# One-hots for the gate matrices, made token by token instead of eight tokens at a time

## What is computed

```
s = einsum('nhpc,hpkc->nhpk', q, sub_keys)            # two sides of 128 scores
ts, ti = top_k(s, 16)
cand_s = ts[:, :, 0, :, None] + ts[:, :, 1, None, :]
cand_i = ti[:, :, 0, :, None] * 128 + ti[:, :, 1, None, :]
best_s, best_p = top_k(cand_s, 16)
idx = take_along_axis(cand_i, best_p)
gate = softmax(best_s)
act = gelu(einsum('nd,nhkd->nhk', x, u[idx]))
out = einsum('nhk,nhkd->nd', gate * act, v[idx])
```

## Time and profile before

| | |
|---|---|
| median of 3 runs | 2251.53 us |
| the profiled execution | 2253.01 us, span 2251.7 us |
| PE busy | 2114.5 us (94%) |
| DVE busy | 1506.8 us (67%) |
| ACT busy | 879.1 us (39%) |
| POOL busy | 714.2 us (32%) |
| DVE instructions | 2554 |
| mean granted clock of PE | 0.971 of 2.4 GHz |

### The profile page before, as it was taken

One profiled execution on the slowest core, in us unless ns is written; L12 is line 12 of the kernel. 1 busy time (PEld: TensorE's weight loads), 2 busy tenths in 40 slices (PEclk: granted clock), 3 DMA queues, 4 the chain that ended last, 5 costly groups with the idle time before them and its releaser, 6 DMA issues.

```text
span 2251.7 us, 31360 instructions
## 1 busy us (share of the span) xinstructions
PE 2114.5 (94%) x12750; PEld 1228.8 (55%) x12827; DVE 1506.8 (67%) x2554; ACT 879.1 (39%) x1057; POOL 714.2 (32%) x540
## 2 busy tenths in 40 slices
PE   6999999999999979999999999999789898999998
PEld 5464664555566646666655555555445464444444
DVE  4557644798989899996788888888674374332002
ACT  5333542333243337675333333333232464434110
POOL 2311001311334342223233333343336302555440
PEclk9999899999999989999999999999799998999999
DMA  6223571226898888889999999999422201322310
GB/s 208 75 75 114 183 266 38 95 75 220 301 340 303 311 301 291 333 326 349 376 373 378 384 372 383 381 381 371 155 75 99 75 20 38 112 92 95 150 38 38
DMA packets 194479, 483.39 MB, mean 215 GB/s; under 512 B 10672, under 2 KB 93648, under 8 KB 188320
## 3 DMA queue, kind: packets, MB, share of 16 engines
q1 hardware_dynamic: 154624, 334.65, 41.5%
q0 software_dynamic: 39712, 146.74, 17.3%
HBM read 428.92 MB, written 52.43 MB: 214 GB/s over the span
## 4 chain that ended last, share of the span: by engine, by line
PE 50%; DVE 28%; DMA 15%; issue 3%; ACT 2%; POOL 1%; SPq 1%; DVEq 0%; ACTq 0%; POOLq 0%
PE psum L568 13%; PE psum L569 13%; PE psum L567 13%; DMA expert_act<-act_dram 12%; DVE weight_low L2060 6%; DVE row_sum L2301 2%; POOL weight_low L2634 1%; DVE hidden_low L2480 1%; DVE expert_act L2475 1%; DVE gated_one_hot_b L2460 1%; DVE one_hot_b L2457 1%; PE psum L788 1%; DVE one_hot_a L2454 1%; DVE rows_a L2288 1%; PE psum L882 1%
## 5 line engine op out<-in xcount | busy, mean ns | idle before, releaser
L567 PE MATMUL psum<-x_high,weight_high 128*128 128x384 bf16 (+3 forms) x1825 | 632.0, 346 | 22.5 <-DVE weight_low L2060 17.2
L568 PE MATMUL psum<-x_low,weight_high 128*128 128x384 bf16 (+3 forms) x1845 | 639.7, 347 | 11.1 <-DVE x_low L1938 5.9
L569 PE MATMUL psum<-x_high,weight_low 128*128 128x384 bf16 (+3 forms) x1844 | 638.7, 346 | 0.6
L1330 ACT ACTIVATE weight_high<-weight_stage 128x4096 bf16<-128x4096 f32 (+2 forms) x100 | 356.3, 3564 | 243.3 <-DMA weight_stage<-peer_v_dram 120.7
L2634 POOL TENSOR_TENSOR weight_low<-weight_stage,weight_high 128x512 bf16<-128x512 f32 (+1 forms) x229 | 300.8, 1348 | 426.2 <-ACT weight_high L1330 426.2
L567 PE MATMUL psum<-hidden_high,weight_high 128*128 128x384 bf16 x1024 | 333.8, 326 | 7.3 <-DVE hidden_low L2480 7.3
L569 PE MATMUL psum<-hidden_high,weight_low 128*128 128x384 bf16 x1024 | 333.8, 326 | 0.0
L568 PE MATMUL psum<-hidden_low,weight_high 128*128 128x384 bf16 x1024 | 333.8, 326 | 0.0
L2060 DVE TENSOR_TENSOR weight_low<-weight_stage,weight_high 128x4096 bf16<-128x4096 f32 x69 | 304.5, 4415 | 11.9 <-ACT weight_high L1330 11.9
L567 PEld LDWEIGHTS psum<-x_high,weight_high 128*128 128x128 bf16 (+1 forms) x1856 | 184.2, 99 | 184.0 <-issue 21.9
L569 PEld LDWEIGHTS psum<-x_high,weight_low 128*128 128x128 bf16 (+1 forms) x1856 | 184.0, 99 | 155.4 <-issue 8.7
(11 more groups left out here) (364 smaller groups left out, 2903.7 us busy)
## 6 DMA issues: line engine op xcount, KB each, us to landing
weight_stage<-peer_u_dram SPq DMA_DIRECT2D x32, 2048.0 KB
weight_stage<-peer_v_dram SPq DMA_DIRECT2D x32, 2048.0 KB
weight_stage<-mlp_w_dram SPq DMA_DIRECT2D x16, 2048.0 KB
weight_stage<-ada_w_dram SPq DMA_DIRECT2D x12, 2048.0 KB
act_dram<-norm_value SPq DMA_DIRECT2D x128, 192.0 KB
gate_dram<-gate_matrices SPq DMA_DIRECT2D x12, 2048.0 KB, 12.0
gates<-gate_dram SPq DMA_DIRECT2D x32, 768.0 KB, 16.2
expert_act<-act_dram SPq DMA_DIRECT2D x32, 768.0 KB
```

The costliest lines, as they stand in the source:

```text
L567: self.nc.tensor.matmul(out, left[0], right[0], start=first, stop=False)
L568: self.nc.tensor.matmul(out, left[0], right[1], start=False, stop=False)
L569: return self.nc.tensor.matmul(out, left[1], right[0], start=False, stop=last)
L1330: nc.scalar.activation(k.block_view(m.w_high, n % SPLITS, n), k.block_view(m.w_stage, n % STAGES, n), ACT.Copy).then_inc(*s.w_high.up(n))
```

## The change

One-hots are made per token. The token's two numbers and its gate are kept as f32 with one value per partition (`pick_t`), and the compare and the product with the gate are one instruction, `tensor_scalar` with two operations, on 128 elements. `right` goes away, and with it the wait for the previous step. The high part of the gate is made by a cast on DVE, followed by a wait and the subtraction. The iota has 128 elements instead of 256 and its cast stands ahead of the wait for the last tile. The operands of the matmuls become contiguous.

```diff
-        self.iota16, self.pick_b = m("iota_picks", [P, TOPK]), m("picks_t_bf16", [P, 4, DT], BF16)
+        self.iota16, self.gate_high, self.gate_low = (
+            m("iota_picks", [P, TOPK]), m("gates_t_high", [P, DT], BF16), m("gates_t_low", [P, DT]))
...
-                        c, y = divmod(4 * q + x, OI)
-                        ins = nc.tensor.matmul(k.psum[:, i, NK * x:NK * (x + 1)], m.left[:, v, c, :, y],
-                                               m.gated[part][:, v, c, :, y], start=part == 0, stop=part == 1)
+                        ins = nc.tensor.matmul(k.psum[:, i, NK * x:NK * (x + 1)], m.left[:, v, 4 * q + x, :],
+                                               m.gated[part][:, v, 4 * q + x, :], start=part == 0, stop=part == 1)
...
-            nc.scalar.activation(m.pick_b[:, 0:3, P * chosen:P * (chosen + 1)],
+            nc.scalar.activation(m.pick_t[:, :, P * chosen:P * (chosen + 1)],
...
-            nc.vector.tensor_tensor(m.pick_b[:, 3, at], k.psum[:, k.bank_of["picks", t], 2 * P:3 * P],
-                                    m.pick_b[:, 2, at], ALU.subtract).then_inc(*s.routed.up("split", t))
+            nc.vector.tensor_copy(m.gate_high[:, at], m.pick_t[:, 2, at]).then_inc(*s.step.up())
+            nc.vector.wait_ge(*s.step.now())
+            nc.vector.tensor_tensor(m.gate_low[:, at], m.pick_t[:, 2, at], m.gate_high[:, at], ALU.subtract).then_inc(
+                *s.routed.up("split", t))
...
         nc.vector.wait_ge(*s.in_iota_keys.at())
+        nc.vector.tensor_copy(m.iota[:, :], m.iota32[:, :]).then_inc(*s.step.up())
+        nc.vector.wait_ge(*s.step.now())
         nc.vector.wait_ge(*s.routed.at("split", ROUTE_TILES[-1]))
-        nc.vector.tensor_copy(m.iota[:, :, :], m.iota32[:, :].unsqueeze(2).to_broadcast([P, NK, OI])).then_inc(
-            *s.step.up())
-        nc.vector.wait_ge(*s.step.now())
-        iota = m.iota[:, :, :].unsqueeze(1).to_broadcast(hots)
         for n in range(HOT_STEPS):
-            v, tokens = n % 2, slice(OC * n, OC * (n + 1))
-            number_a, number_b, gate_high, gate_low = (
-                m.pick_b[:, x, tokens].rearrange("p (c n) -> p c n", n=OI).unsqueeze(2).to_broadcast(hots)
-                for x in range(4))
+            v = n % 2
             if n >= 2:
                 nc.vector.wait_ge(*s.gate_mats.at(n - 2, OC // 4 - 1))
-            nc.vector.tensor_tensor(m.left[:, v], iota, number_a, ALU.is_equal).then_inc(*s.step.up())
-            if n >= 1:
-                nc.vector.wait_ge(*s.hot.at(n - 1))
-            nc.vector.tensor_tensor(m.right[:, :, :, :], iota, number_b, ALU.is_equal).then_inc(*s.step.up())
-            nc.vector.wait_ge(*s.step.now())
-            nc.vector.tensor_tensor(m.gated[0][:, v], m.right[:, :, :, :], gate_high, ALU.mult).then_inc(*s.step.up())
-            nc.vector.tensor_tensor(m.gated[1][:, v], m.right[:, :, :, :], gate_low, ALU.mult).then_inc(*s.hot.up(n))
+            for x in range(OC):
+                token = slice(OC * n + x, OC * n + x + 1)
+                nc.vector.tensor_scalar(m.left[:, v, x, :], m.iota[:, :], m.pick_t[:, 0, token], None, ALU.is_equal)
+                nc.vector.tensor_scalar(m.gated[0][:, v, x, :], m.iota[:, :], m.pick_t[:, 1, token],
+                                        m.pick_t[:, 2, token], ALU.is_equal, ALU.mult)
+                ins = nc.vector.tensor_scalar(m.gated[1][:, v, x, :], m.iota[:, :], m.pick_t[:, 1, token],
+                                              m.gate_low[:, token], ALU.is_equal, ALU.mult)
+            ins.then_inc(*s.hot.up(n))
```

More of the change, by code:

```diff
@@ L41 @@
 TC = 32
-OC, OI = 8, 2
+OC = 8
 ROW_TILE, DT = QT - 1, SEQ - P
@@ L266, in __init__ @@
         hot = Map(nc, top)
-        one_hots = [P, 2, OC // OI, NK, OI]
-        self.left, self.right = hot("one_hot_a", one_hots, BF16), hot("one_hot_b", one_hots[:1] + one_hots[2:], BF16)
+        one_hots = [P, 2, OC, NK]
+        self.left = hot("one_hot_a", one_hots, BF16)
         self.gated = [hot(f"gated_one_hot_b_{part}", one_hots, BF16) for part in range(2)]
@@ L283, in __init__ @@
             self.mod_rows[:, PICKS * x:PICKS * (x + 1)] for x in range(4))
-        self.row_sum = Map(nc, m.at)("row_sum", [P, D])
+        after_index = Map(nc, m.at)
+        self.row_sum, self.pick_t = after_index("row_sum", [P, D]), after_index("picks_t", [P, 3, DT])
         self.keys = m("sub_keys", [P, 2 * PH, NK])
         m = Map(nc, free + 2 * 4 * D)
-        self.iota32, self.iota = m("iota_keys", [P, NK]), m("iota_bf16", [P, NK, OI], BF16)
+        self.iota32, self.iota = m("iota_keys", [P, NK]), m("iota_bf16", [P, NK], BF16)
         m = Map(nc, top)
@@ L2438, in gate_matrices @@
     def gate_matrices(self):
         nc, s, m = self.nc, self.s, self.m
-        hots = [P, OC // OI, NK, OI]
         nc.vector.wait_ge(*s.in_iota_keys.at())
+        nc.vector.tensor_copy(m.iota[:, :], m.iota32[:, :]).then_inc(*s.step.up())
+        nc.vector.wait_ge(*s.step.now())
         nc.vector.wait_ge(*s.routed.at("split", ROUTE_TILES[-1]))
-        nc.vector.tensor_copy(m.iota[:, :, :], m.iota32[:, :].unsqueeze(2).to_broadcast([P, NK, OI])).then_inc(
-            *s.step.up())
-        nc.vector.wait_ge(*s.step.now())
```

## The result

The changed kernel takes 2362.66 us (median of 4 runs, 2353.74 to 2364.61) against 2251.55 us before: 1.0478 times as long, 95% interval 1.0462 to 1.0495, or 104 to 111 us more. (The ratio is the record's, taken over all runs; the quotient of the two medians is 1.0493, inside the interval.) The forecast was 2362. The profiled execution took 2364.61 us, with a span of 2363.3.

What follows compares the result with a forecast made beforehand. DVE sets the one-hot stage, PE close behind; -5.4 - 1.2 + 115.9 + 0.46 + 1 = +110.8 us on the profiled 2253.0 us gives 2363.8, as median 2362 us. Range 2312 to 2404, with 0.80 inside.

Steps and rivals of the forecast that it cites:

- Who sets the stage: One-hot stage, 836 to 1040 us: DVE sets the pace, busy 196.9 of 204 us; PE has 17 us idle.
- The price of a value per partition: New one-hot instructions: each value per partition adds about 0.06 us; fixed part 0.133 us with one, 0.193 with two.
- rival 1: Gated one-hots: two values per partition cost no more than one, 46 us less, 2316 us; chance 0.10.
- rival 2: One-hots: per-partition values fetched while the instruction ahead streams, costing nothing; 2239 to 2248 us; chance 0.07.
- The elements: New one-hots: 128 bf16 elements take 0.033 us, half the f32 price of 0.066.
- Rival 3: One-hots: bf16 gives nothing, 2400 us (chance 0.10), or one element at a time, 2477 us (0.05).
- The sum for a step: One-hots of 8 tokens on DVE: 4.94 us instead of 2.53; 48 steps 237.3 instead of 121.4, 115.9 us more.
- The small parts ahead of the first one-hot: DVE before the one-hots: gate split 0.78 us more, iota's cast moved into idle time -0.32, together +0.46 us.
- PE's lag behind the last one-hot: End of the one-hot stage: PE's lag of 1.2 us behind DVE's last one-hot goes.
- The clock: PE in the one-hot stage: granted clock dips after gaps, costing 1 us for the tile following the last step.
- Rival 4: One-hot stage: PE stays at 1.2 GHz throughout and becomes the bound, 65 us on top, 2427 us; chance 0.05.
- Nothing is given back behind the stage: Expert stage: PE has no gap, 107.95 of 108 us busy, so a later stage end moves the kernel's end equally.

Runs made afterwards that it cites:

- the run with the better order: The kernel before, with the one-hot of b made ahead of that of a and the iota's cast ahead of the last split's wait: 2245.39 us, ratio 0.9974.

## Why the prediction was right, point by point

**Who sets the stage: right.** DVE is busy for 312.25 of 314 us, PE waits 95.5 us for it, and twice as many matmuls make the stage 1.5 us longer. Two of the signs that the prediction named were off in size, though: PE is busy for 68% of the stage, not 60%, and waits 95.5 us, not well over 100. I counted PE's work at full clock; it took 27.6 us more at the clock that it got.

**The price of a value per partition: right.** Without the second value and its operation 49 us went (46 forecast for rival 1), with constants throughout the whole cost went, and the starts moved by 0.06 us per value: 0.10, 0.16, 0.22. Rival 1 (two for the price of one) and rival 2 (hidden behind the instruction ahead) fall with these starts. The Trainium skill ("VectorE: DVE Perf Modes", section "The TRN2 errata — SBUF-src ops pay a fixed extra latency per instruction") has 58 cycles and the elements over the rate, an estimate of 94 ns for an instruction here, by which the change would have been a gain. The traces are near it for constants, where the starts are 0.104 us apart, and have 1.7 and 2.4 times as much with one and two values per partition.

**The elements: right.** 0.033 us was taken by analogy from two-source rows; the f32 form gave 39 us more where 38 were worked out for the slower rate. Rival 3 falls.

**The sum for a step: 1.5% too high.** 4.94 forecast, 4.87 measured in the mean. DVE's stage (first one-hot to the instruction behind the last) went from 203.4 to 309.6 us, 106.2 more where 115.9 - 5.4 = 110.5 were forecast. Added up over the timelines, the 1152 new instructions took 233.8 us, not 237.3: each start came 0.003 us sooner than forecast (0.163 and 0.223 for 0.166 and 0.226). The 192 old ones took 122.0 us without the waits for PE, not 121.4, as the mean step was 2.54 where the one measured was 2.53. These 3.5 and 0.6 us are the whole of the difference.

**The small parts ahead of the first one-hot: one mechanism wrong.** I put the cast of the iota into DVE's idle time ahead of the last split (-0.32 us). That idle time stands ahead of the gate's cast, in `route`, and the iota's cast comes behind the subtraction in DVE's order; so it still stands on the path:

```profile
841.15 0.23 DVE L2436 CAST gates_t_high<-picks_t 128x128 bf16<-128x128 f32 x1 [1.58 <-ACT picks_t L1656]
841.41 0.29 DVE L2438 TENSOR_TENSOR gates_t_low<-picks_t,gates_t_high 128x128 f32<-128x128 f32 x1
841.62 0.22 DVE L2444 CAST iota_bf<-iota_keys 128x128 bf16<-128x128 f32 x1
841.87 0.25 DVE L2453 TENSOR_SCALAR one_hot_a<-iota_bf,picks_t 128x128 bf16<-128x128 bf16 x1
```

What it gave came from elsewhere: it starts 0.21 us behind the start of the subtraction instead of 0.40, and the first one-hot follows it after 0.25 instead of 0.32 us, 0.26 less in all. The size was nearly right by luck. From the cast of the picks' iota (below) to the first one-hot it is all the same 1.0 us longer where 0.46 was forecast; 0.35 of that is DVE's wait for ScalarE in the brackets, 1.58 against 1.23 us, and as the run with the better order has 1.58 there too, this is not the change's.

**PE's lag behind the last one-hot: wrong by 1.8 us, which the clock explains.** I let the lag of 1.2 us vanish and gave 1 us for the clock. In fact PE begins with the last one-hots at 1153.30, 1.7 us after DVE ends (1151.56), since the filler tile ahead of them ran at the lower clock for a part: its matmuls start 0.32 us apart from 1147.28 to 1151.44, and 0.16 from 1151.67 on. At 0.16 throughout, these 13 spacings would have been 2.1 us shorter and PE would have been done first.

```profile
1150.16 0.53 PE L569 MATMUL psum<-x_high,weight_high 128*128 128x384 bf16 x1
1150.48 0.53 PE L570 MATMUL psum<-x_low,weight_high 128*128 128x384 bf16 x1
...
1151.84 0.33 PE L569 MATMUL psum<-x_high,weight_high 128*128 128x384 bf16 x1
1152.00 0.33 PE L570 MATMUL psum<-x_low,weight_high 128*128 128x384 bf16 x1
```

The two entries together were -0.2 us in the sum and +0.6 in the trace. With three times the matmuls, at full clock, PE begins there 0.6 us after DVE ends.

**The clock: right in kind.** It fell in the gaps and came back in the work, down to the lower level where PE stood: 0.50 in 896 to 902 us, in which it had no matmul, 1.00 again in 908 to 914. Rival 4, a stage at 1.2 GHz throughout, did not come.

```profile
896.00:902.00 6.00, 0.00 (x0) 0.00 (x0) 6.00 (x26) 0.00 (x0) 0.00 (x0) 0.50 0.67 216
...
908.00:914.00 6.00, 5.63 (x46) 3.54 (x43) 6.00 (x26) 2.74 (x4) 0.94 (x1) 1.00 0.91 363
```

**The total agrees better than its parts, by luck.** The profiled execution is 111.6 us longer in its span. Of this 4.9 us were there at the cast of the picks' iota (399.0 us before, 403.9 after; one line by its source in each kernel), which runs ahead of everything that the change touches:

```profile
L2367 DVE CAST iota_places<-iota_picks x1: 293/293/293, 403.9 to 403.9; 128x256 bf16<-128x256 f32 x1
```

In ten profiled executions that point lies between 397.0 and 404.4 us, with no order by kernel (the changed kernel with more matmuls has 397.1). It is scatter between executions, as are the 11 us between the changed kernel's fastest and slowest run. The other terms: 1.0 from there to the first one-hot (0.46 forecast), 106.2 for the stage, 0.6 for PE's lag, -1.0 for all that is behind. So the change costs some 107 us in this pair of traces, against 110.8 forecast (the ratio of all runs, 1.0478, gives 108 too); the interval of the ratio, 104 to 111, holds both. That 2362 met the median of 2362.66 to within 1 us is luck.

**Nothing is given back behind the stage: right.** From PE's start on the last one-hots to the end it is 1210.0 us, and 1211.0 before; 1 us is within the scatter between executions.

## What to carry to other kernels

Ask of a small VectorE instruction first what it reads: here a constant added nothing to the fixed 0.07 us and a value per partition cost 0.06 us, nearly twice what the elements of the whole instruction cost. Trading a few large instructions at 0.53 ns per element for many small ones at 0.26 pays only while the fixed parts stay below what the rate saves; here 192 instructions became 1152 and the rate gain was worth some 0.035 us on each. On an engine that sets the pace, look for waits on a result made by the instruction just ahead, and put another independent one between them.

## What the runs showed of the hardware

Rows of other stages, on f32 and other sizes, priced the new instructions to 2%: the starts of `tensor_scalar` on 128 bf16 elements are 0.10, 0.16 and 0.22 us apart with none, one and two values per partition, a second operation costs nothing, and another 128 elements in the same instruction cost 0.035. What I had not expected is how evenly this held with 1152 such instructions in a row; there was no added cost from their number, and GpSimd's 36 asks for rows in the stage took as long in all as before (56.9 us busy against 55.8 for 35), though the small instructions ran at 0.26 ns per element beside them. With constants in place of the values that is not quite so: in the run with constants GpSimd is busy for 66.7 us of its 200.3 us stage with 35 asks, and 20 or so of the 1152 starts are 0.18 to 0.20 us apart instead of 0.10. Whether the two belong together no run here tests.
